# Reordering the start of a two-block transformer kernel, and zero-padding its rotary keys

## The reference

```
# block 1
h = rmsnorm(x, g_pre)
qkv, z_a, b_raw, a_raw, glu_in, z_b, gates = split(h @ w_in)      # b_raw, a_raw: 16 columns each
beta, g_log = sigmoid(b_raw), -exp(a_log) * softplus(a_raw + dt_bias)
o_a = gated_delta(conv4(qkv), g_log, beta) ...                    # needs the decays
u   = conv31(glu(glu_in), w_dw) + b_dw ; layernorm(ln_g, ln_b) ; silu ...
x   = x + rmsnorm((gate_a * (o_a @ w_br_a) + gate_b * (u @ w_br_b)) @ w_out) ; x = x + per-layer part
# block 2
q_a, c_kv, k_rope, ... = split(rmsnorm(x) @ w_in_2)
k_rope, q_rope = rope(k_rope, cos, sin), rope(q_rope, cos, sin)   # 64 wide, one k_rope for all heads
scores = q_nope . k_nope + q_rope . k_rope                        # per head: 128 + 64 deep
out = x + rmsnorm((softmax(scores) @ v, gated, + short convolution branch) @ w_out_2)
```

## Time and profile before

| | |
|---|---|
| time, median of 3 runs | 2634.55 us (2634.34 to 2637.29) |
| time of the profiled execution | 2635.0 us |
| its span, first to last instruction | 2633.2 us |
| PE busy | 2519.0 us, 96% |
| DVE / ACT / POOL busy | 1653.3 / 1161.8 / 170.4 us |
| mean granted TensorE clock | 0.989 |
| transfers | 469.66 MB, mean 178 GB/s |

### The profile page before, as it was taken

One profiled execution on the slowest core, in us unless ns is written; L12 is line 12 of the kernel. 1 busy time (PEld: TensorE's weight loads), 2 busy tenths in 40 slices (PEclk: granted clock), 3 DMA queues, 4 the chain that ended last, 5 costly groups with the idle time before them and its releaser, 6 DMA issues.

```text
span 2633.2 us, 32737 instructions
## 1 busy us (share of the span) xinstructions
PE 2519.0 (96%) x12351; PEld 2106.2 (80%) x12351; DVE 1653.3 (63%) x2127; ACT 1161.8 (44%) x1484; POOL 170.4 (6%) x244
## 2 busy tenths in 40 slices
PE   4999999988999999999999988999999999999997
PEld 4878888877878878888887877878888888888886
DVE  3699998678576666745656564555554544465554
ACT  4444444455352533524445454443444444443443
POOL 2000000153010100101000010000000000000000
PEclk9999999999999999999999999999999999999999
DMA  4666666445242333637665544555555666675563
GB/s 156 198 188 225 199 212 206 160 148 173 96 144 97 112 129 104 218 126 255 230 207 185 191 168 136 184 175 183 183 179 179 208 203 194 198 267 195 187 224 112
DMA packets 225973, 469.66 MB, mean 178 GB/s; under 512 B 12062, under 2 KB 12119, under 8 KB 224663
## 3 DMA queue, kind: packets, MB, share of 16 engines
q1 hardware_dynamic: 213098, 418.57, 48.1%
q0 software_dynamic: 12768, 49.59, 5.4%
HBM read 445.05 MB, written 23.07 MB: 178 GB/s over the span
## 4 chain that ended last, share of the span: by engine, by line
PE 70%; DVE 3%; ACT 2%; issue 1%; POOL 0%; DVEq 0%; ACTq 0%; POOLq 0%
PE acc L2007 58%; PE aux L2135 4%; PE aux L2037 1%; DVE w_lo L1315 1%; PE aux L2401 1%; PE aux L2400 1%; PE aux L2140 1%; PE aux L2216 1%; PE aux L2220 0%; DVE cy L1529 0%; ACT w_hi L773 0%; PE aux L2205 0%; PE aux L2215 0%; PE acc L2307 0%; ACT qT L992 0%
## 5 line engine op out<-in xcount | busy, mean ns | idle before, releaser
L1315 DVE TENSOR_TENSOR w_lo<-raw,w_hi 128x1024 fp32r<-128x1024 f32 (+1 forms) x790 | 974.0, 1236 | 830.0 <-ACT w_hi L773 819.6
L773 ACT CAST w_hi<-raw 128x1024 fp32r<-128x1024 f32 (+1 forms) x790 | 827.4, 1051 | 1271.1 <-PE acc L2007 1251.4
L2007 PE MATMUL acc<-w_hi,r1h 128*128 128x512 f32 (+1 forms) x1920 | 762.8, 397 | 17.1 <-issue 10.1
L2007 PE MATMUL acc<-w_lo,r1h 128*128 128x512 f32 (+1 forms) x1920 | 747.8, 389 | 0.0
L2007 PE MATMUL acc<-w_hi,r1l 128*128 128x512 f32 (+1 forms) x1920 | 747.2, 389 | 0.0
L2007 PE MATMUL acc<-w_hi,r2h 128*128 128x512 f32 x1216 | 477.2, 392 | 2.2 <-DVE w_lo L1315 1.9
L2007 PE MATMUL acc<-w_hi,r2l 128*128 128x512 f32 x1216 | 473.5, 389 | 0.0
L2007 PE MATMUL acc<-w_lo,r2h 128*128 128x512 f32 x1216 | 473.3, 389 | 0.0
L2007 PEld LDWEIGHTS acc<-w_hi,r1h 128*128 128x128 f32 x1920 | 363.0, 189 | 92.5 <-issue 15.7
L2007 PEld LDWEIGHTS acc<-w_hi,r1l 128*128 128x128 f32 x1920 | 362.5, 189 | 75.6
L2007 PEld LDWEIGHTS acc<-w_lo,r1h 128*128 128x128 f32 x1920 | 363.2, 189 | 69.9 <-issue 1.0
(11 more groups left out here) (426 smaller groups left out, 1630.2 us busy)
## 6 DMA issues: line engine op xcount, KB each, us to landing
raw<-in_w_in SPq DMA_DIRECT2D x264, 1024.0 KB, 5.0
raw<-in_w_out SPq DMA_DIRECT2D x32, 1024.0 KB, 5.0
raw<-in_w_br_b SPq DMA_DIRECT2D x16, 1024.0 KB, 5.1
raw<-in_w_br_a SPq DMA_DIRECT2D x16, 1024.0 KB, 6.1
raw<-in_w_ple_gate SPq DMA_DIRECT2D x16, 1024.0 KB, 5.0
raw<-in_w_o_mla SPq DMA_DIRECT2D x16, 1024.0 KB, 4.9
raw<-in_w_o_conv SPq DMA_DIRECT2D x16, 1024.0 KB, 5.0
raw<-in_w_q_b SPq DMA_DIRECT2D x8, 1024.0 KB, 5.1
```

Of the source, the lines that this page charges most:

```text
L773: nc.scalar.copy(w_hi[:, h % HL, 0:n], raw[:, k % RAW, x * HALF:x * HALF + n]).then_inc(hi_ready, 1)
L1315: V.tensor_tensor(w_lo[:, h % HL, 0:n], raw[:, k % RAW, x * HALF:x * HALF + n], w_hi[:, h % HL, 0:n].bitcast(F32), ALU.subtract).then_inc( ...
L2007: ins = T.matmul(acc[:, s, x, 0:n], a[:, kt0 + k, xs_], w[:, h % HL, at], start=start and k == 0 and m == 0, stop=stop and k == kts - 1 an ...
```

## The change

It has these parts:

1. **Rows.** `crow` becomes 128 partitions by 7 slots of 128 values: a parameter row of 2048 stands on 16 partitions. Five small sets of rows (`g_pre`, `ln_g`, `ln_b`, `pre_norm_g_2`, `conv_w_2`) are loaded first; the others (`w_dw`, `b_dw`, `w_conv_qkv` and three gains) behind the first weight block. The transposes become 1 early and 6 later; `pc` is filled in two parts (`columns()` is the later one).
2. **x.** Two loads of 1 MB; ACT squares the lower and DVE the upper half of each row; POOL's `rsqrt` stands ahead of the masks; `x` is scaled in four column pieces (`x_scaled`).
3. **First block.** GLU0 shrinks to one block (8 halves), the other is GLU1, and BA stands between them. PE transposes two groups of `x`, then runs half `hl` of GLU0 (which needs group `hl` alone) and transposes group `hl + 2` behind it. SP loads GLU0's block ahead of the later rows and BA.
4. **Decays.** `decays_in`, `decays_log`, `decays_end` on DVE, `decays_softplus`, `decays_exp`, `decays_kend` on ACT and `log_decays` on PE hang on halves 1 to 7 of GLU1.
5. **Angles.** The rotary angles go to half 0 of GT3 on DVE, the sines to half 1 on ACT, the cosines to half 3 on DVE.
6. **Keys.** `krT` becomes two tiles of 128 rows: tile 0 has the keys on rows 0 to 63 and zeros below, tile 1 zeros and then the keys. L2401 is then 128 rows deep, with both heads of `qrT` as its weights. `amask` moves to another place in memory, and `wq4` is copied with a stride of three values.

```diff
-            sp.dma_start(xt[:], tok(t["x"][0])).then_inc(sem("x_landed"), 16)
-            sp.dma_start(crow[R_DW:R_DW + TAPS, :], t["w_dw"][0]).then_inc(sem("rows_landed"), 16)
...
-            load(PH["BA"], 0, w_in[:, :, C_BA:C_BA + 2 * HEADS], shape=(KT, 2 * HEADS))
-            load_block(PH["GLU0"], 0, w_in, C_GLU + D)
-            load_block(PH["GLU0"], 1, w_in, C_GLU)
+            for x in range(TT):
+                sp.dma_start(xt[:, x], tok(t["x"][0])[:, x]).then_inc(sem(f"x_landed{x}"), 16)
+            for r, name in ((R_GPRE, "g_pre"), (R_LNG, "ln_g"), (R_LNB, "ln_b")):
+                sp.dma_start(place(r, 1), rows(t[name])).then_inc(sem("gains_rows_landed"), 16)
...
+            load_block(PH["GLU0"], 0, w_in, C_GLU + D)
+            sp.dma_start(crow[:, 0:whole], taps[0:whole * P].rearrange("(s p) c -> p s c", p=P)).then_inc(sem("rows_landed"), 16)
...
+            load(PH["BA"], 0, w_in[:, :, C_BA:C_BA + 2 * HEADS], shape=(KT, 2 * HEADS))
+            load_block(PH["GLU1"], 0, w_in, C_GLU)
@@ ACT, the start
+            act.wait_ge(sem("rstd_ready"), RSTD_X)
+            x_scaled(0)
+            split(0)
+            act.wait_ge(sem("prep_ready"), PREP_GPRE)
+            x_hi(0)
+            x_hi(1)
+            split(1)
+            x_scaled(1)
+            split(2)
@@ DVE, the start (after the norm's sum and the copy of the gains)
+            dve.wait_ge(sem("rstd_ready"), RSTD_X)
+            x_scaled(0)
+            split(0)
+            x_lo(0)
+            x_lo(1)
+            split(1)
+            x_scaled(1)
+            split(2)
@@ DVE (ACT the same with x_hi), GLU0; then GLU1
             for hl in range(ph.hn):
+                if hl + 2 < KT // 2:
+                    x_lo(hl + 2)
+                if hl in (1, 3):
+                    x_scaled(2 + hl // 2)
                 ahead(ph, hl)
@@ PE
+            x_transposed(0)
+            x_transposed(1)
             ph = PH["GLU0"]
             for hl in range(ph.hn):
+                pe.wait_ge(sem("op_lo"), 2 * OP_HT + hl + 1)
                 model_half(ph, hl, 0, r1)
+                if hl + 2 < KT // 2:
+                    x_transposed(hl + 2)
+            narrow(PH["BA"], r1, 2 * HEADS, 3)
+            ph = PH["GLU1"]
+            for hl in range(ph.hn):
+                model_half(ph, hl, 0, r1)
+                if hl == 0:
+                    pe.wait_ge(sem("prep_ready"), PREP_NARROW)
+                    narrow_tr(narrow_t, 2 * HEADS, 3).then_inc(sem("rows_tr"), 1)
                 if hl == 1:
+                    rows_transposed()
+                if hl == 4:
                     log_decays()
@@ ACT, GT3
                 if hl == 3:
                     act.wait_ge(sem("conv_done"), NJ)
                     upad_copy(NJ - 1)
+                if hl == 1:
+                    rope_sines()
@@ DVE, GT3
                 if hl == 0:
                     c.link(V.tensor_copy(pcw[:], pc[:, LAST * CT:, 0:TAPS + 1]))
+                    rope_angles()
+                if hl == 3:
+                    rope_cosines()
@@ DVE, KVA
-                    sig(V.tensor_copy(krT[:], X[:, 3, 0:TOK]), "krT_ready", 1)
+                    c.inc(V.memset(krT[ROPE:2 * ROPE, 0], 0.0))
+                    c.inc(V.memset(krT[0:ROPE, 1], 0.0))
+                    c.inc(V.tensor_copy(krT[0:ROPE, 0], X[0:ROPE, 3, 0:TOK]))
+                    c.wait()
+                    sig(V.tensor_copy(krT[ROPE:2 * ROPE, 1], X[ROPE:2 * ROPE, 3, 0:TOK]), "krT_ready", 1)
@@ PE, FC
-                            half = slice(h % 2 * ROPE, (h % 2 + 1) * ROPE)
...
-                                ins = T.matmul(X[:, h, at], qrT[half, h // 2, x * P:(x + 1) * P], krT[half, 0:keys], start=False, stop=True)
+                                ins = T.matmul(X[:, h, at], qrT[:, h // 2, x * P:(x + 1) * P], krT[:, h % 2, 0:keys], start=False, stop=True)
```

More of the change, by code:

```diff
@@ L125, in plan @@
     order = [
+        ("GLU0", 1, [full] * 4, 1),
         ("BA", 1, [(1, KT * 2 * HEADS)], 0),
-        ("GLU0", 1, [full] * 8, 2),
+        ("GLU1", 1, [full] * 4, 1),
         ("GLU", 3, [full] * 16, 4),
@@ L360, in build_layer @@
             c3 = s1("c3", [P, CT, TOK])
-            krT = s1("krT", [P, TOK])
-            amask = s1("amask", [P, SCORES])
+            krT = s1("krT", [P, 2, TOK])
             mx, nmx, den, rec = [s1(n, [P, TT, GH]) for n in ("mx", "nmx", "den", "rec")]
@@ L370, in build_layer @@
             wc2 = s1("wc2", [P, CT, TAPS2])
+            amask = s1("amask", [P, SCORES])
             assert nc.sbuf_base <= tail_at + 2 * D * 4
@@ L428, in _, with rows @@
[L428 to L431, removed]
+            for x in range(TT):
+                sp.dma_start(xt[:, x], tok(t["x"][0])[:, x]).then_inc(sem(f"x_landed{x}"), 16)
+            def rows(src):
+                return src.rearrange("r (k c) -> (r k) c", c=P)
@@ new lines, in _ @@
+            load_block(PH["GLU0"], 0, w_in, C_GLU + D)
+            taps, whole = rows(t["w_dw"][0]), TAPS // ROW_SLOT
+            sp.dma_start(crow[:, 0:whole], taps[0:whole * P].rearrange("(s p) c -> p s c", p=P)).then_inc(sem("rows_landed"), 16)
+            sp.dma_start(place(whole * ROW_SLOT, TAPS % ROW_SLOT), taps[whole * P:]).then_inc(sem("rows_landed"), 16)
+            sp.dma_start(place(R_BDW, 1), rows(t["b_dw"])).then_inc(sem("rows_landed"), 16)
+            short = rows(t["w_conv_qkv"][0])
@@ L781, in sig, with x_scaled @@
                 act.wait_ge(sem(name), value)
[L784 to L792, removed]
+            for x in range(TT):
+                act.wait_ge(sem(f"x_landed{x}"), 16)
+                sig(A(sz0[:].rearrange("p t n -> p (t n)"), xt[:, x, 0:D // 2], ACT.Square, accum_out=stat[:, 40 + x:41 + x]), "row_sq", x + 1)
+            def x_scaled(q):
+                A(xt[:, 0, q * NB:(q + 1) * NB], xt[:, 0, q * NB:(q + 1) * NB], ACT.Copy, scale=stat[:, 2:3]).then_inc(sem("xn0_ready"), 1)
             def stationary_hi(dst, kt, bank, scale_col, tr_sem, tr_value, hi_sem, hi_value):
@@ L1456, in _ @@
             for hl in range(ph.hn):
+                if hl + 2 < KT // 2:
+                    x_lo(hl + 2)
+                if hl in (1, 3):
+                    x_scaled(2 + hl // 2)
                 ahead(ph, hl)
-            glu(ph, 1, 0, freed(ph, 0), None)
+            ahead(PH["BA"], 0)
+            narrow_copy()
+            ph = PH["GLU1"]
+            for hl in range(ph.hn):
+                ahead(ph, hl)
+                if hl == 1:
+                    decays_in()
+                if hl == 2:
+                    columns()
+                if hl == 3:
+                    decays_log()
+                if hl == 6:
+                    decays_end()
+            glu(ph, 0, 0, freed(PH["GLU0"], 0), None)
             ph = PH["GLU"]
```

269 lines of the change are left out of this document (154 added, 115 removed).

## The result

The changed kernel takes 2603.78 us, median of 4 runs (2602.93 to 2606.69), against 2635.63 for the kernel before (4 runs, 2634.34 to 2637.29). The ratio is 0.9879, with a 95% interval of 0.9867 to 0.9892: 31.9 us or 1.2% less, and clear of the noise. Predicted were 2602 and a range of 2596 to 2614. The profiled execution took 2606.69 us, 2605.0 of them span; that is 3 us above the median.

What follows compares the result with a forecast made beforehand. PE, busy 96% of the span, was taken as the bound, so gains lay in its idle start and slow score matmuls. -21.9 - 11.8 + 0.9 = -32.8 on 2635.0 us gave 2602.2, said as 2602; range 2596 to 2614.

Steps and rivals of the forecast that it cites:

- Part 1: Start of the kernel: PE's first real matmuls begin sooner, less what the rearrangement costs later; -21.9 us.
- The first half: First half of GLU0: starts at about 16.1 us instead of PE's first real matmul at 40.90; -24.8 us.
- The clock: Start: GLU0's first half meets the half clock that BA met before, about the same loss; zero.
- Six groups of transposes: GLU0: six groups of four x transposes now stand between PE's halves; +3.3 us, bounds 2.7 and 5.4.
- The late rows' transposes: Start: six transposes of parameter rows that now come later on PE; +0.7 us.
- The wait of 1.13: PE's wait at 60.00 us, where ACT had been held up by the decays, should go; -1.1 us.
- Part 2: Attention scores: with all matmuls 128 deep a round takes 5.3 us instead of 8.24; -11.8 us over four rounds.
- Part 3: GT3's start: the angles on DVE delay w_lo and stall PE, ACT waits for them; +0.9 us, bounds 0.5 and 3.
- (a): Scores: padding brings nothing, the extra time has another cause; 2614 us, chance 0.08.
- (b): Start: transfers still hold the weights back until near 22 us, 12 us of gain gone; 2614 us, chance 0.07.
- (c): Start: 1.2 GHz holds from the first half through GLU1, +49.5 us, giving 2652; chance 0.05, of which 0.02 slower.
- (d): Convolution phases: DVE is the limit there, PE catches up and the start's gain is lost; no chance of its own.

Runs made afterwards that it cites:

- angles early: Changed kernel with the rotary angles and sines moved to the last half of GLU1 and the cosines to GT3's half 0: 2603.05 us.
- grouped keys: Changed kernel with unpadded 64-row keys and score matmuls ordered by depth, four of 128 rows and then four of 64, per key length: 2601.40 us.
- keys undone: Changed kernel with the zero padding of the keys taken out, score matmuls alternating 128 and 64 rows deep as before: 2615.27 us.
- x first: Changed kernel with x scaled, transposed and split whole before the first half of GLU0, all else left: 2603.22 us.
- unused matmuls: Changed kernel with 64 unused matmuls before the first transpose and 8 behind the first x transposes: 2604.86 us; also with late small loads, grouped scores, earlier angles: 2602.51.

## Why the prediction was right, point by point

**Part 1, the start: -21.9 predicted, -20.2 measured** (95.77 to 75.58). The mechanism was right. The terms that differ:

- The first half began at 18.54, not 16.1: +2.4. x landed at 10.55 where I took 9.0 (bounds 8.0 to 10.6), since POOL's small loads are under way at that moment, and not the rows or BA's pieces that I had blamed; with them moved it landed at 8.77 and the half began at 15.30. ACT then waited 1.45 us for the first weights, which I had called there in time: they were behind the same slow stretch. DVE's scaling at 14.13 had waited for the copy of the gains, another piece of it.
- The clock, put at zero: the half ran at the pace of 1.2 GHz until about 22 us, 18.54 to 23.05, 4.5 us instead of 2.75, +1.8. BA before took 6.75 us (40.90 to 47.65) and now, at full pace, 5.45: -1.3. Net +0.5.
- Six groups of transposes: 0.35 us and 0.1 on the matmul behind them, 2.7 in all, my lower bound; predicted 3.3, so -0.6.
- A wait of 0.51 before BA's small transposes of before is gone, as half 0 of GLU1 now covers it: not in the sum, -0.6. The late rows' transposes took 0.57 and 0.1, as put. The wait of 1.13 went, as put, and the decays cost no wait.

Sum of the differences: 2.4 + 0.5 - 0.6 - 0.6 = 1.7, and -21.9 + 1.7 = -20.2.

Where those 20 us come from, by position in the experiments: the layout of the rows brings 9.1, of which one load's 31 rows split in two bring 5.2 (6.5 at BA's start), and running x beside the first block 0.9, within the spread of u and not seen in the time. The remaining 10 lie between two kernels that both convert all of x before their first matmul: the one before with the new rows (u at 86.71) and the changed one with the overlap undone (76.48). x landed at about the same time in both, 10.38 and 10.79. The norm's sum on DVE and the first transposes of x stand at

```profile
17.42 0.16 DVE L1389 TENSOR_TENSOR stat<-stat 128x2 f32<-128x2 f32 x1
22.17 6.48 PE L2078 MATMUL aux<-ident,xt 128*128 128x128 f32 x32 [6.75 <-ACT xt L805]
```

in the first, and in the second at

```profile
12.06 0.16 DVE L1399 TENSOR_TENSOR stat<-stat 128x2 f32<-128x2 f32 x1
14.49 3.58 PE L2145 MATMUL aux<-ident,xt 128*128 128x128 f32 x16 [1.18 <-DVE xt L1405]
```

So 5.4 us lie ahead of the sum. There the first kernel has ACT alone square x, until 15.1, and DVE's work on the rows next, until 17.3; the second shares the squares, which end at 12.0, and has the rows' work behind. Another 2.3 us lie between the sum and the transposes (inverse root, and scaling in pieces), 1.3 in the transposes and the conversion, and some 1.2 behind the first matmul, where waits of 0.51 and 1.17 are gone and the late transposes of rows (0.7) have come. This is read from two traces; no kernel changed one of these parts alone. "x beside the first weight block", the part that looks largest, is the one for which no gain can be shown.

**Part 2, the scores: -11.8 predicted.** The distance between both traces' same PE instructions grows by 3.1 us a round, 12.5 in four; undone it costs 11.5, alone it brings 12.8. Right, and by the mechanism put down: the 16 matmuls take 5.05 us where I had 5.3, with no extra left. Only the reading beside it was too wide: "the trace does not agree" with overlap holds for alternating order alone.

**Part 3, GT3: +0.9 predicted, +1.0 measured.** A wait of 0.68 us was added where I put 0.8, and ACT stood idle before the sines, as foreseen. By position it is 1.0: the distance between both traces is 20.3 before GT3 and 19.3 at the next transposes of `sz` (439.35 and 420.09), and with the angles earlier it stays at 20.3.

**Total.** The sum by position is -20.2 - 12.5 + 1.0 = -31.7; the medians differ by 31.9. The profiled execution shows 28.4 behind the last round. Between 1050 and 1600 us it lost 4, which the sum leaves out: PE waited 1.5 us for a late transfer, and the granted clock was low for longer. Windows of the same work, first before, then changed (length, busy time by engine, PE clock, DMA share, GB/s):

```profile
1520.00:1620.00 100.00, 89.21 (x439) 74.66 (x440) 57.03 (x90) 55.40 (x92) 7.39 (x12) 0.92 0.49 169
```
```profile
1500.00:1600.00 100.00, 88.02 (x417) 73.32 (x418) 56.63 (x92) 53.08 (x89) 6.59 (x12) 0.88 0.47 158
```

I had expected the changed kernel run again to be free of this, near 2603.5. It was not: its profiled execution took 2605.75, again the slowest of four, with a clock of 0.90 there and a wait of 0.9 for the same transfer (`r1l<-delta_branch_spill`). That wait is 1.4 us with the angles early, 0.4 with grouped keys, 0.3 in the kernel before with the new rows, 0.2 with the keys undone, and absent in the other traces: the one before, those with the small loads late, but also that with x first and those with unused matmuls. So it goes with no single edit. Whether the new start makes this loss likelier, or it varies by execution, stays open; 2 to 3 us may hang on it.

**The rivals.** (a) Padding brings nothing: refuted by undoing it (+11.5) and by adding it alone (-12.8). (b) Transfers gate the start: refuted at the size I gave; 400 GB/s is back from 12 us on and only 1.45 us were lost on weights. (The short pieces are 112, not 80, as the 112 rows of their one transpose show.) A small form of it is true, and POOL's loads are its cause. (c) The low clock stays: refuted; matmuls are 0.23 us apart from 22 us on, with a group of transposes behind each of the first six halves. The rule of the Trainium skill that the prediction puts beside it, that transposes do not bring up the full clock, does not hold in the kernel before: its 32 transposes of x, with nothing else on PE, start 0.21 us apart from 31.48 on and 0.11 apart from 36.85 on. (d) DVE takes part 1 back: refuted; right before GT3 the distance is still 20.3.

## What to carry to other kernels

Read the transfer rates of the start by the microsecond. Give a load of few long rows an outer size that divides by 16, or split it (31 into 16 and 15 was worth 8 us by run here), and keep small broadcast loads away from the load that all wait for (2 to 4 us). Where matmuls of two depths alternate, group them by depth before padding the shallow ones: 8.24, 5.05 and 4.61 us a round for alternating, padded and grouped. Before building a finer overlap, undo it on the way and see what the end of the stage says: a start 4 us sooner was worth 0.9 by position and nothing in the time, since its pieces moved in between.

## What the runs showed of the hardware that I had not expected

- fp32 matmuls of 64 rows on alternating halves overlap when they are neighbours: eight instructions of 256 columns in 1.06 us, against 1.92 at 128 rows; at 128 columns 0.65 against 0.98. Between matmuls of 128 rows nothing of it shows.
- Four small loads on POOL's queue take SP's 1 MB loads from about 400 down to between 112 and 227 GB/s in the slices from 7 to 11 us; with these loads later the same slices show 374 to 414. Which of the four does it, no run shows.
- The recorded clock reads 1.00 until its first change, even while the matmuls' distance is that of 1.2 GHz. In this window of the changed kernel (columns as above) the record says 1.00, and the timeline has the matmuls 0.42 to 0.43 us apart:

```profile
20.00:21.00 1.00, 1.00 (x4) 0.81 (x3) 1.00 (x2) 0.69 (x1) 0.87 (x3) 1.00 1.06 399
```

  So at the start of a trace the pace is to be read from start times. Later the two agree: BA in the kernel before, at 0.50, has its matmuls 0.21 us apart, and 0.11 at 1.00.
- Transposes alone brought PE to the full pace, in the kernel before from 36.85 us on. Then PE stood idle for 2.99 us, and BA met the low clock again.
